# One-core backbone block: modulation rows as unsplit products on four column quarters, re-queued pieces, reordered head work, x loaded first

## The chip, the cores and the metric

The kernel runs on one NeuronCore of one Trainium2 chip. The metric is device time in microseconds (us), lower is better. The kernel before takes 2216.18 us, the median of three runs (2215.4 to 2218.75).

## What is computed

Two layers of a diffusion backbone over 256 context tokens and 512 latent tokens, 1024 channels wide, in float32. Both layers read six modulation vectors (shift, scale and gate, twice), made from a conditioning vector `c` for the latent tokens and `c_ctx` for the context tokens:

```python
def adaln(cvec, w, b):                       # w: (1024, 6144) per layer
    m = jax.nn.silu(cvec) @ w + b
    return jnp.split(m[:, None, :], 6, axis=-1)

for i in range(DEPTH):                       # DEPTH = 2
    sh1, sc1, g1, sh2, sc2, g2 = adaln(c, ada_w[i], ada_b[i])
    hl = modulate(rms_norm(xl, norm1_g[i]), sh1, sc1)      # h * (1 + scale) + shift
    # layer 0: gated linear recurrence of 8 heads, forward and backward (hgrn2_mixer)
    # layer 1: windowed attention with sinks (window_gqa_mixer)
    xl = xl + g1 * ol
    xl = xl + g2 * conv_ffn(modulate(rms_norm(xl, norm2_g[i]), sh2, sc2), ...)
    # the context tokens take the same steps in layer 0
return rms_norm(xl, final_norm_g)
```

The modulation weights are 2 x 1024 x 6144 floats, 48 MB of the traffic. The kernel holds them as 24 rows (12 in each layer) of 512 outputs; a row has four pieces, and a piece has two blocks of 128 inputs by 512 outputs.

## The kernel before, in words

Activations lie with channels on the partitions and tokens along the row. A large product goes over 204 weight tiles of 1024 x 128 channels: 40 for the eight recurrence heads (five for each), 8 for the mixer's output, 68 for the feed-forward of layer 0, then 12, 8 and 68 in layer 1. Each weight tile is read into one of three raw buffers `WR`, split on ScalarE into a high part `WH` (L787) and on VectorE into the rest `WL` (L1086), both in the one-pass type fp32r. TensorE makes three products for each block (L400 to L402): high by high, high by low and low by high. Products of plain float32 operands also occur (L527, L713, L722). The trace shows each of these as two MATMUL records, so its counts are twice the program's.

Every engine runs its own instruction list in order and waits on semaphores. SyncE's list holds all loads: it issues the load of weight tile t once `tile_done` says that tile t-3 was used, and `PIECES` says how many modulation pieces are loaded behind each tile's load. A raw piece arrives as two halves of 128 x 512 in two buffers `ada_raw`. GpSimd splits each half into `ada_high` (L357) and `ada_low` (L359). The load of the next half waits in SyncE's list for `piece_split`, so every later load in that list stands behind it.

A recurrence head is one head step. On TensorE it has ten half tiles of the *next* head's projection (numbered n = 0 to 9, 24 products of 384 columns each). Between them come the products of the current head: eight rounds of scores (level -1 behind n = 2, level k behind n = k + 3; L525 and L527), the key-value products and outputs of the head before (n = 0 and 1), its norm (sums at n = 2, `spread` L498 at n = 3), and the modulation products (L453, L454; n = 5 to 8) with the turn of a finished row into a column (L446, n = 9). Each round of scores waits until VectorE has taken the one before out of PSUM (`take`, L1294). VectorE's list for a head step is: forget gates, states of the head before, `head_out` of the head before (L1317, L1319; it waits for `spread`), the take of level -1, then for each level merging of keys (L1255, L1256), merging of queries (L1266, L1267), take, totals (L1282), with the weight splits `split_low` between them. The eighth head step has no projection of a next head; the mixer's output products fill it.

The feed-forward of layer 0 does the other 12 modulation rows, one piece in the middle of each tile (`ada_tiles`). At the start of the kernel the first four rows are read in `AD0`, split by ScalarE, VectorE and GpSimd (L938, L1143, L373) and multiplied (L479), before the first norm and the first tiles.

One modulation row before: `silu_p` holds the high and the low part of both conditioning vectors, 4 columns in all. For each of the 8 blocks there are two one-pass products, 16 in all, which write 4 partitions of `MB`. ScalarE copies them to `ada_row`, and four small products with `fold` add the parts and put the row across the partitions.

Of the kernel before, what the change touches and what calls it, by code (L numbers as in the profile page):

```python
# [19 lines left out]
F32 = mybir.dt.float32  # L20
# [78 lines left out]
def trunk(nc, small_in, x_in, ada_in, w_in, ident_in, masks_in, rope_in, rot_in, tri_in, out):  # L99
    ctx = ExitStack()  # L100
    with ctx:
# [15 lines left out]
        AR = [sb(f"ada_raw{i}", [P, 512]) for i in range(2)]  # L117
        AH = [sb(f"ada_high{i}", [P, 512], F32R) for i in range(2)]
        AL = [sb(f"ada_low{i}", [P, 512], F32R) for i in range(2)]
# [5 lines left out]
        silu_c = sb("silu_c", [P, KC, 2])  # L125
        sig_c = sb("sig_c", [P, KC, 2])
        silu_p = sb("silu_p", [P, KC, 4], F32R)
        ada_row = sb("ada_row", [4, 512])
        fold = sb("fold", [4, 2])
# [22 lines left out]
        with ExitStack() as s:  # L152
            AD0 = sb("AD0", [P, 4 * ADA_FIRST, 1024], F32, s)
        with ExitStack() as s:
# [11 lines left out]
            O1 = sb("O1", [P, TOK], F32, s)  # L166
            KL = [sb(f"KL{i}", [P, TOK], F32, s) for i in range(2)]
        with ExitStack() as s:
            GH = sb("GH", [P, max(GROUPS), TOK], F32R, s)
            GL = sb("GL", [P, max(GROUPS), TOK], F32R, s)  # L170
            UW = (GRID_H + 2) * (GRID_W + 2)
            UP = [sb(f"UP{i}", [P, UW + CTX + 2], F32, s) for i in range(2)]
            ACC = [sb(f"ACC{i}", [P, TOK], F32, s) for i in range(2)]
        with ExitStack() as s:
# [10 lines left out]
            rope = sb("rope", [P, 2, LAT], F32, s)  # L185
# [23 lines left out]
        ada0_in = [sem(f"ada0_in{i}") for i in range(4 + ADA_FIRST - 1)]  # L209
        ada0_hi, ada0_lo, ada0_lo_pool, ada0_used = sem("ada0_hi"), sem("ada0_lo"), sem("ada0_lo_pool"), sem("ada0_used")  # L210
        w_in_done = [sem(f"w_in_done{i}") for i in range(NB)]
        piece_in = [sem(f"piece_in{i}") for i in range(2)]
# [3 lines left out]
        piece_hi, piece_split = sem("piece_hi"), sem("piece_split")  # L216
        piece_used = sem("piece_used")
        sig_ready, silu_ready, lb_shifted = sem("sig_ready"), sem("silu_ready"), sem("lb_shifted")
        ada_copied, ada_turned, ada_ready = sem("ada_copied"), sem("ada_turned"), sem("ada_ready")
# [20 lines left out]

        BACK, FORE = 0, 1

# [16 lines left out]

        def first_part(t, n):  # L260

            return t[:, :, :].rearrange("p c t -> p (c t)")[:, 1024 * (n % 6):1024 * (n % 6 + 1)]
# [44 lines left out]
        def _(sp):  # L307
            sp.dma_start(small[:, :], small_in).then_inc(small_in_done, 16)
            for n in range(4):
                sp.dma_start(AD0[:, n, :], ada_in[n]).then_inc(ada0_in[n], 16)  # L310
            sp.dma_start(ident[:, :], ident_in).then_inc(ident_in_done, 16)
            for g in range(1, ADA_FIRST):
                sp.dma_start(AD0[:, 4 * g:4 * g + 4, :], ada_in[4 * g:4 * g + 4].rearrange("n p f -> p n f")).then_inc(ada0_in[3 + g], 16)
                if g == 1:
                    sp.dma_start(X[:, :, :], x_in).then_inc(x_in_done, 16)
            sp.dma_start(mask_stage, masks_in).then_inc(masks_in_done, 16)

            raw = Tally()
# [29 lines left out]
        def _(pool):  # L348
            pieces = Tally()

            def split_piece():
                for f in range(2):
                    pieces.add()
                    pool.wait_ge(piece_in[f], pieces.half(0, 16))
                    if pieces.some(2):
                        pool.wait_ge(piece_used, pieces.now(2))
                    pool.tensor_scalar(AH[f][:, :], AR[f][:, :], 1.0, 0.0, ALU.mult, ALU.add).then_inc(piece_hi, 1)  # L357
                    pool.wait_ge(piece_hi, pieces.now())
                    pool.tensor_tensor(AL[f][:, :], AR[f][:, :], AH[f][:, :].bitcast(F32), ALU.subtract).then_inc(piece_split, 1)  # L359

# [9 lines left out]
            for g in range(ADA_FIRST):  # L370
                p = 4 * g + 3
                pool.wait_ge(ada0_hi, p + 1)
                pool.tensor_tensor(first_part(HL, p), AD0[:, p, :], first_part(HH, p).bitcast(F32), ALU.subtract).then_inc(ada0_lo_pool, 1)  # L373
            for n in range(4 * ADA_FIRST, 4 * ADA_GROUPS):
                split_piece()
                if n == 4 * ADA_FIRST + 28:
                    split_heads()

        @block.tensor
        def _(pe):  # L380
# [60 lines left out]
            def ada_turn():  # L441
# [3 lines left out]
                for m in range(4):  # L445
                    last = mm(MB[:, 512 + 2 * m:514 + 2 * m], ada_row[:, m * P:(m + 1) * P], fold[:, :], start=True, stop=True)  # L446
                last.then_inc(ada_turned, 1)

            def ada_piece(k):
                for f in range(2):  # L450
                    pieces.add()
                    pe.wait_ge(piece_split, pieces.now())
# [1160 lines left out]
```

## Time and profile before

| | |
|---|---|
| time, median of 3 runs | 2216.18 us |
| time of the profiled execution | 2217.54 us |
| its span, first to last instruction | 2215.5 us |
| TensorE matmul busy | 2034.7 us, 92% |
| VectorE busy | 1305.8 us, 59% |
| ScalarE busy | 704.2 us, 32% |
| GpSimd busy | 395.8 us, 18% |
| mean granted TensorE clock | 0.946 of full speed |

The profiled execution has 2.0 us outside its span. In the profile PE is TensorE's matmul, PEld its weight load, DVE VectorE, ACT ScalarE, POOL GpSimd and SPq the list of loads. A matmul's duration includes the time in the pipeline, so the start-to-start distance of two neighbours is what one costs in a row.

### The profile page before, as it was taken

To read this page: it belongs to the slowest core of one execution; us is meant where nothing else is said; L and a number is where in the kernel's file an instruction comes from. 1 tells how busy PE (TensorE), PEld (TensorE's weight loads), DVE (VectorE), ACT (ScalarE), POOL (GpSimd) and SP (SyncE) were. 2 spreads that over 40 slices of the span, in tenths; PEclk is the share of its full clock that TensorE was granted. 3 is DMA by queue.
4 is the path that set the end of the run, shared out by engine and by line. 5 is a ranking of instruction groups with operands and counts; after the bars stand their busy time and mean duration, and the time that the engine had idled before them with its cause. 6 is when DMAs were issued, how large, how long until landed. Compare 5 with 4: busy or idle time off the path is not lost.

```text
span 2215.5 us, 26437 instructions
## 1 busy us (share of the span) xinstructions
PE 2034.7 (92%) x10776; PEld 1695.0 (77%) x10776; DVE 1305.8 (59%) x2043; ACT 704.2 (32%) x1065; POOL 395.8 (18%) x342
## 2 busy tenths in 40 slices
PE   5999989899978889999999999799899879999997
PEld 2989889888877768888888888675565567777775
DVE  5555465474566367744774376575355468568485
ACT  5323322323322233221232133345335333233232
POOL 1021222122062004533553352000000000000000
PEclk7999989999989989999999999899989999999998
DMA  6121211212110113323333233210010022232232
GB/s 254 48 76 53 72 58 49 75 48 76 49 58 29 57 52 101 114 95 96 114 104 96 95 111 89 71 58 1 14 44 1 29 76 85 85 94 89 86 95 95
DMA packets 56856, 165.85 MB, mean 75 GB/s; under 512 B 6176, under 2 KB 6560, under 8 KB 56608
## 3 DMA queue, kind: packets, MB, share of 16 engines
q1 hardware_dynamic: 56736, 164.17, 23.3%
q8 instruction: 85, 1.39, 0.3%
q14 instruction: 35, 0.29, 0.0%
HBM read 162.05 MB, written 2.10 MB: 74 GB/s over the span
## 4 chain that ended last, share of the span: by engine, by line
PE 73%; DVE 16%; ACT 4%; DMA 3%; issue 2%; POOL 1%; SPq 0%; DVEq 0%; POOLq 0%
PE slot L400 18%; PE slot L402 17%; PE slot L401 17%; DVE ACC L1403 6%; PE MA L527 4%; PE slot L722 3%; DVE WL L1086 3%; DMA WR<-in_w 2%; PE MB L453 2%; PE MB L454 1%; ACT WH L787 1%; PE slot L713 1%; PE MB L498 1%; PE MB L446 1%; DMA AD<-in_ada 1%
## 5 line engine op out<-in xcount | busy, mean ns | idle before, releaser
L400 PE MATMUL slot<-HH,WH 128*128 128x256 f32 (+2 forms) x2016 | 724.8, 360 | 42.8 <-DVE ACC L1411 14.1
L401 PE MATMUL slot<-HL,WH 128*128 128x256 f32 (+2 forms) x2016 | 710.8, 353 | 0.0
L402 PE MATMUL slot<-HH,WL 128*128 128x256 f32 (+2 forms) x2016 | 710.2, 352 | 0.0
L400 PEld LDWEIGHTS slot<-HH,WH 128*128 128x128 f32 x2016 | 388.3, 193 | 106.6 <-issue 49.1
L1086 DVE TENSOR_TENSOR WL<-WR,WH 128x1024 fp32r<-128x1024 f32 x204 | 292.1, 1433 | 278.4 <-ACT WH L787 276.8
L401 PEld LDWEIGHTS slot<-HL,WH 128*128 128x128 f32 x2016 | 388.1, 193 | 41.4 <-issue 2.2
L402 PEld LDWEIGHTS slot<-HH,WL 128*128 128x128 f32 x2016 | 386.3, 192 | 38.4
L787 ACT ACTIVATE WH<-WR 128x1024 fp32r<-128x1024 f32 x204 | 215.1, 1055 | 415.8 <-DMA WR<-in_w 415.6
L1403 DVE SCALAR_TENSOR_TENSOR ACC<-UP,cw,ACC 128x512 f32<-128x512 f32 x352 | 291.9, 829 | 8.6
L357 POOL TENSOR_SCALAR ada_high<-ada_raw 128x512 fp32r<-128x512 f32 x160 | 129.1, 807 | 904.1 <-DMA ada_raw<-in_ada 454.5
L359 POOL TENSOR_TENSOR ada_low<-ada_raw,ada_high 128x512 fp32r<-128x512 f32 x160 | 236.7, 1479 | 13.3
L400 PE MATMUL slot<-GH,WH 128*128 128x512 f32 (+1 forms) x528 | 192.0, 364 | 8.4 <-DVE GL L1416 8.4
L402 PE MATMUL slot<-GH,WL 128*128 128x512 f32 (+1 forms) x528 | 190.9, 362 | 0.0
L401 PE MATMUL slot<-GL,WH 128*128 128x512 f32 (+1 forms) x528 | 190.5, 361 | 0.0
L527 PE MATMUL MA<-QQ,KL 128*128 128x128 f32 x672 | 102.8, 310 | 51.2 <-DVE PS L1294 51.1
L527 PEld LDWEIGHTS MA<-QQ,KL 128*128 128x128 f32 x672 | 96.9, 219 | 56.1 <-issue 56.0
L400 PEld LDWEIGHTS slot<-GH,WH 128*128 128x128 f32 x528 | 100.5, 190 | 27.0 <-DVE GL L1416 9.7
L991 ACT ACTIVATE ACC<-ACC 128x768 f32<-128x768 f32 (+1 forms) x44 | 32.5, 739 | 272.3 <-DVE ACC L1403 272.3
L401 PEld LDWEIGHTS slot<-GL,WH 128*128 128x128 f32 x528 | 100.7, 191 | 16.8
L402 PEld LDWEIGHTS slot<-GH,WL 128*128 128x128 f32 x528 | 100.7, 191 | 16.5
L873 ACT ACTIVATE KL<-KK 128x384 f32<-128x384 f32 x112 | 53.3, 524 | 127.8 <-DVE KK L1256 124.1
L722 PE MATMUL slot<-PT,AV 128*64 128x512 f32 x144 | 74.8, 670 | 1.4 <-ACT PT L1033 1.4
(182 smaller groups left out, 2159.9 us busy)
## 6 DMA issues: line engine op xcount, KB each, us to landing
WR<-in_w SPq DMA_DIRECT2D x204, 512.0 KB, 3.6
ada_raw<-in_ada SPq DMA_DIRECT2D x160, 256.0 KB, 2.6
AD<-in_ada SPq DMA_DIRECT2D x3, 2048.0 KB, 22.9
X<-in_x SPq DMA_DIRECT2D x1, 3072.0 KB, 19.2
AD<-in_ada SPq DMA_DIRECT2D x4, 512.0 KB, 7.0
out<-Y SPq DMA_DIRECT2D x8, 256.0 KB, 2.2
Y<-in_masks SPq DMA_DIRECT2D x1, 512.0 KB, 25.6
rope<-in_rope SPq DMA_DIRECT2D x1, 512.0 KB, 3.4
```

The source lines that it names most:

```text
L357: pool.tensor_scalar(AH[f][:, :], AR[f][:, :], 1.0, 0.0, ALU.mult, ALU.add).then_inc(piece_hi, 1)
L359: pool.tensor_tensor(AL[f][:, :], AR[f][:, :], AH[f][:, :].bitcast(F32), ALU.subtract).then_inc(piece_split, 1)
L400: mm(SLOT[s][:, po], WH[w % NB][:, k, :], hi[:, k, to], start=(k == 0), stop=False)
L401: mm(SLOT[s][:, po], WH[w % NB][:, k, :], lo[:, k, to], start=False, stop=False)
L402: last = mm(SLOT[s][:, po], WL[w % NB][:, k, :], hi[:, k, to], start=False, stop=(k == kn - 1))
L453: mm(MB[0:4, 0:512], silu_p[:, 2 * k + f, :], AH[f][:, :], start=(k == 0 and f == 0), stop=False)
L527: last = mm(MA[:, chunk(c)], KL[n % 2][:, t], of_level(QQ[b], c * P, P, 2 ** n), start=True, stop=True)
L722: last = mm(SLOT[1][64 * half:64 * half + 64, 0:512], AV[:, c, 64 * half:64 * half + 64], PT[v % 2][:, j, :, :].rearrange("p r q -> p (r q ...
L787: go(WH[t % NB][:, :, :], WR[t % NB][:, :, :], ACT.Copy).then_inc(w_hi_done, 1)
L873: last = go(k, half(KK[b], plane, s, plane), ACT.Copy)
L1086: tt(WL[t % NB][:, :, :], WR[t % NB][:, :, :], WH[t % NB][:, :, :].bitcast(F32), ALU.subtract).then_inc(w_split, 1)
L1403: ins = stt(acc, lat[:, dy:dy + GRID_H, dx:dx + GRID_W], cw[b][:, k:k + 1], acc, ALU.mult, ALU.add)
```

## The change

1. **Unsplit products.** `silu_w` holds the two conditioning vectors in float32, in columns 0 and 1 of 32, the rest zero. A row is 8 plain float32 products of a 128 x 32 stationary operand with a 128 x 512 block. Blocks 0 to 3 write the four column quarters of the array, partitions 0, 32, 64 and 96 of `MB`, and blocks 4 to 7 add to them. `fold`, now 128 x 2, adds the quarters in the turn. GpSimd's splits and `piece_split` are gone, and GpSimd keeps `split_heads` only.
2. **Re-queued pieces.** A piece is one load of 128 x 1024 into one of four buffers, it waits for `pair_used` (TensorE's use of the pair that the buffer held), and is queued behind other tiles: in a head step two pieces each behind two neighbouring tile loads. TensorE does a pair of pieces at once: n = 6 and n = 8 of a head step, and every other tile in the feed-forward.
3. **Start.** x is loaded first, then the pieces. The squares of x are made before the rows, and the norm's sums and reciprocal between the third row and the fourth. `split_low` of the first three tiles moves behind the first scaled chunk. The splits of the first four rows are gone.
4. **Head step.** `head_out` moves from ahead of the take of level -1 (the masked copy of the diagonal scores, `take(LEVELS)`) to behind `merge_keys(0)`. The buffer `O1` is gone; `V` takes its place.

```diff
-            after, n, t = {}, 4 * ADA_FIRST, 7
+            after, n, t = {}, 4 * ADA_FIRST, 5
             for h in range(HEADS - 1):
-                for j in range(5):
-                    after[t + j - 1] = 2 * (j in (2, 3))
+                after[t + 1], after[t + 2] = 2, 2
                 t += 5
-            after[t - 1] = 4
+            after[t + 1], after[t + 2] = 2, 2
...
             def load_piece(n):
-                for f in range(2):
-                    if raw.some(1):
-                        sp.wait_ge(piece_split, raw.now(1))
-                    raw.add()
-                    sp.dma_start(AR[f][:, :], ada_in[n, :, f * 512:(f + 1) * 512]).then_inc(piece_in[f], 16)
+
+                i = n - 4 * ADA_FIRST
+                if i >= 4:
+                    sp.wait_ge(pair_used, i // 2 - 1)
+                sp.dma_start(AR[i % 4][:, :, :], ada_in[n].rearrange("p (f o) -> p f o", f=2)).then_inc(piece_in[i % 4], 16)
...
-            def ada_piece(k):
-                for f in range(2):
-                    pieces.add()
-                    pe.wait_ge(piece_split, pieces.now())
-                    mm(MB[0:4, 0:512], silu_p[:, 2 * k + f, :], AH[f][:, :], start=(k == 0 and f == 0), stop=False)
-                    mm(MB[0:4, 0:512], silu_p[:, 2 * k + f, :], AL[f][:, :], start=False, stop=(k == 3 and f == 1)).then_inc(piece_used, 1)
-                if k == 3:
+            def ada_products(src, k):
+
+                for f in range(4):
+                    c = 2 * k + f
+                    last = mm(MB[32 * f:32 * f + 32, 0:512], silu_w[:, c, :], src(f), start=(k == 0), stop=(k == 2))
+                return last
+
+            def ada_pair(k):
+
+                i = pieces.now()
+                pieces.add(2)
+                for j in range(i, i + 2):
+                    pe.wait_ge(piece_in[j % 4], 16 * (j // 4 + 1))
+                ada_products(lambda f: AR[(i + f // 2) % 4][:, f % 2, :], k).then_inc(pair_used, 1)
+                if k == 2:
                     rows.add()
...
-                    if 5 <= n < 9:
-                        ada_piece(n - 5)
+                    if n in (6, 8):
+                        ada_pair(n - 6)
...
                 scaled(0)
+                if early:
+                    split_low(tile.now() + AHEAD)
...
                 if tail:
                     token_rstd(0)
-                    head_out(h - 1)
                 head.add()
                 take(LEVELS)
                 for n in range(LEVELS):
                     merge_keys(b, n)
+                    if tail and n == 0:
+                        head_out(h - 1)
```

SyncE's list, the loads from the first head step on, before (`WR` are weight tiles, `ada_raw` halves of pieces):

```order
16 L331 DMA WR2<-in_w 128x1024 [waits tile_done]
17 L326 DMA ada_raw0<-in_ada 128x512
18 L326 DMA ada_raw1<-in_ada 128x512
19 L326 DMA ada_raw0<-in_ada 128x512 [waits piece_split]
20 L326 DMA ada_raw1<-in_ada 128x512 [waits piece_split]
21 L331 DMA WR0<-in_w 128x1024 [waits tile_done]
22 L326 DMA ada_raw0<-in_ada 128x512 [waits piece_split]
23 L326 DMA ada_raw1<-in_ada 128x512 [waits piece_split]
24 L326 DMA ada_raw0<-in_ada 128x512 [waits piece_split]
25 L326 DMA ada_raw1<-in_ada 128x512 [waits piece_split]
26 L331 DMA WR1<-in_w 128x1024 [waits tile_done]
```

The same place now, with the pieces of the second head step:

```order
22 L325 DMA WR2<-in_w 128x1024 [waits tile_done]
23 L325 DMA WR0<-in_w 128x1024 [waits tile_done]
24 L325 DMA WR1<-in_w 128x1024 [waits tile_done]
25 L325 DMA WR2<-in_w 128x1024 [waits tile_done]
26 L320 DMA ada_raw0<-in_ada 128x1024 [waits pair_used]
27 L320 DMA ada_raw1<-in_ada 128x1024 [waits pair_used]
28 L325 DMA WR0<-in_w 128x1024 [waits tile_done]
29 L320 DMA ada_raw2<-in_ada 128x1024 [waits pair_used]
30 L320 DMA ada_raw3<-in_ada 128x1024 [waits pair_used]
31 L325 DMA WR1<-in_w 128x1024 [waits tile_done]
```

Before, WR0 and WR1 (rows 21 and 26) stand behind halves that wait for a split. Now the loads in front of a weight tile wait for a pair's products alone.

VectorE's list at the start of the second head step, before (`O1`, `Y` are the output of the head before, `PS` the scores, `KK1` and `QQ1` keys and queries):

```order
149 L1159 RECIPROCAL rstd6<-std6 128x6 [waits std_ready]
150 L1317 TENSOR_TENSOR O1<-O1,MB 128x768 [waits rstd_spread]
151 L1319 TENSOR_TENSOR Y<-Y,O1 128x768 [waits dve_step]
152 L1294 COPY_PREDICATED PS<-masks,MA 128x384 [waits scores_read,scores_done]
153 L1294 COPY_PREDICATED PS<-masks,MA 128x384
154 L1255 TENSOR_TENSOR KK1<-KK1,FD1 128x384 [waits keys_mixed,dve_step]
155 L1256 TENSOR_TENSOR KK1<-KK1,FD1 128x384
156 L1266 TENSOR_TENSOR QQ1<-QQ1,FD1 128x384 [waits scores_done]
```

And now:

```order
141 L1114 RECIPROCAL rstd6<-std6 128x6 [waits std_ready]
142 L1265 COPY_PREDICATED PS<-masks,MA 128x384 [waits scores_read,scores_done]
143 L1265 COPY_PREDICATED PS<-masks,MA 128x384
144 L1226 TENSOR_TENSOR KK1<-KK1,FD1 128x384 [waits keys_mixed,dve_step]
145 L1227 TENSOR_TENSOR KK1<-KK1,FD1 128x384
146 L1288 TENSOR_TENSOR V<-V,MB 128x768 [waits rstd_spread]
147 L1290 TENSOR_TENSOR Y<-Y,V 128x768 [waits dve_step]
148 L1237 TENSOR_TENSOR QQ1<-QQ1,FD1 128x384 [waits scores_done]
```

The take and the first merge of keys no longer stand behind the wait for `rstd_spread`.

## Rows read from the trace of the kernel before

**Rows 1.** The page: busy times, and the chain that ended last, by engine.

```profile
PE 2034.7 (92%) x10776; PEld 1695.0 (77%) x10776; DVE 1305.8 (59%) x2043; ACT 704.2 (32%) x1065; POOL 395.8 (18%) x342
PE 73%; DVE 16%; ACT 4%; DMA 3%; issue 2%; POOL 1%; SPq 0%; DVEq 0%; POOLq 0%
```

**Rows 2.** Stretches: length, busy by engine, clock, DMA share, GB/s.

```profile
16.00:34.00 18.00, 8.90 (x29) 4.55 (x30) 8.12 (x8) 11.43 (x14) 4.33 (x2) 0.62 1.00 409
144.00:620.00 476.00, 433.82 (x2726) 412.86 (x2725) 262.86 (x487) 144.54 (x212) 96.14 (x97) 0.95 0.19 60
620.00:644.00 24.00, 20.12 (x117) 18.18 (x116) 14.60 (x26) 6.48 (x12) 12.85 (x14) 0.93 0.35 109
664.00:690.00 26.00, 22.81 (x149) 20.41 (x147) 16.52 (x29) 6.83 (x11) 5.49 (x5) 0.93 0.00 1
690.00:710.00 20.00, 15.42 (x91) 11.74 (x90) 18.59 (x34) 3.29 (x7) 10.46 (x10) 0.91 0.25 79
800.00:1420.00 620.00, 616.23 (x3455) 519.86 (x3453) 384.43 (x444) 164.24 (x209) 233.46 (x192) 0.99 0.32 98
```

**Rows 3.** TensorE's waits in 144:620, then 620:690: total, times, longest.

```profile
PE MA L527 <- DVE PS L1294: 40.7, 12, 4.3
...
PE MA L527 <- DVE PS L1294: 7.0, 2, 3.9
```

**Rows 4.** Timeline of SyncE's list: start, length, what, count.

```profile
146.08 2.30 SPq L326 DMA_DIRECT2D ada_raw<-in_ada  x2
148.42 34.29 SPq L331 DMA_DIRECT2D WR<-in_w  x4
```

**Rows 5.** Timeline, VectorE and TensorE, first kind of stall.

```profile
153.52 1.52 DVE L1086 TENSOR_TENSOR WL<-WR,WH 128x1024 fp32r<-128x1024 f32 x1 [6.78 <-ACT WH L787]
...
158.03 2.90 PE L527 MATMUL MA<-QQ,KL 128*128 128x128 f32 x12 [3.57 <-DVE PS L1294]
167.24 1.50 PE L527 MATMUL MA<-QQ,KL 128*128 128x128 f32 x12
```

**Rows 6.** Timeline, VectorE and TensorE, second kind of stall.

```profile
198.35 0.95 DVE L1317 TENSOR_TENSOR O<-O,MB 128x768 f32<-128x768 f32 x1 [6.48 <-PE MB L498]
...
200.22 1.04 DVE L1294 COPY_PREDICATED PS<-masks,MA 128x384 f32<-128x384 uint8 x2
...
201.40 2.90 PE L527 MATMUL MA<-QQ,KL 128*128 128x128 f32 x12 [3.09 <-DVE PS L1294]
```

**Rows 7.** Timeline, TensorE, a modulation piece between two half tiles.

```profile
930.04 0.40 PE L453 MATMUL MB<-ada_high,silu_p 128*4 128x512 f32 x1
930.27 0.39 PE L454 MATMUL MB<-ada_low,silu_p 128*4 128x512 f32 x1
...
930.73 0.40 PE L454 MATMUL MB<-ada_low,silu_p 128*4 128x512 f32 x1
930.97 0.40 PE L400 MATMUL slot<-HH,WH 128*128 128x512 f32 x1
```

**Rows 8.** The chain in order of time: plain float32 products of 512 columns.

```profile
1513.71 3.58 PE slot L722 x8
1525.40 4.43 PE slot L722 x10
```

**Rows 9.** Timeline of the start, TensorE, VectorE and ScalarE.

```profile
28.52 3.90 ACT L938 ACTIVATE HH<-AD 128x1024 fp32r<-128x1024 f32 x4 [3.54 <-DMA AD<-in_ada]
45.39 0.59 ACT L945 ACTIVATE ada_row<-MB 4x512 f32<-4x512 f32 x1 [3.46 <-PE MB L479]
47.12 0.17 DVE L1126 TENSOR_TENSOR ada<-MB,small 128x8 f32<-128x8 f32 x1 [2.35 <-PE MB L446]
49.14 3.49 DVE L1086 TENSOR_TENSOR WL<-WR,WH 128x1024 fp32r<-128x1024 f32 x3
55.96 2.19 DVE L1181 SCALAR_TENSOR_TENSOR Y<-X,coef,MB 128x256 f32<-128x256 f32 x4 [3.02 <-PE MB L498]
59.58 0.66 PE L400 MATMUL slot<-HH,WH 128*128 128x384 f32 x1 [3.66 <-DVE HL L1188]
```

More of the change, by code:

```diff
@@ L116, in trunk @@
         WH = [sb(f"WH{i}", [P, KC, P], F32R) for i in range(NB)]
[L117 to L119 removed]
+        AR = [sb(f"ada_raw{i}", [P, 2, 512]) for i in range(4)]
         ident = sb("ident", [P, P])
@@ L173, in trunk @@
             ACC = [sb(f"ACC{i}", [P, TOK], F32, s) for i in range(2)]
+            row2 = sb("row2", [P, 512], F32, s)
         with ExitStack() as s:
@@ L368, in split_heads @@
                     pool.tensor_tensor(HL[:, h, :], Y[:, h, :], HH[:, h, :].bitcast(F32), ALU.subtract).then_inc(early_lo, 1)
[L370 to L377, printed above, removed]
+            split_heads()
         @block.tensor
@@ L445, in ada_turn @@
                 for m in range(4):
-                    last = mm(MB[:, 512 + 2 * m:514 + 2 * m], ada_row[:, m * P:(m + 1) * P], fold[:, :], start=True, stop=True)
+                    last = mm(MB[:, 512 + 2 * m:514 + 2 * m], ada_row(rows.now(1))[:, m * P:(m + 1) * P], fold[:, :], start=True, stop=True)
                 last.then_inc(ada_turned, 1)
-            def ada_piece(k):
-                for f in range(2):
-                    pieces.add()
-                    pe.wait_ge(piece_split, pieces.now())
-                    mm(MB[0:4, 0:512], silu_p[:, 2 * k + f, :], AH[f][:, :], start=(k == 0 and f == 0), stop=False)
-                    mm(MB[0:4, 0:512], silu_p[:, 2 * k + f, :], AL[f][:, :], start=False, stop=(k == 3 and f == 1)).then_inc(piece_used, 1)
-                if k == 3:
+            def ada_products(src, k):
[10 more added lines that the diff above has]
+                if k == 2:
                     rows.add()
@@ L463, in ada_tiles @@
                         half_tile(j % 2, 0, hi, lo, kn)
[L464 removed]
+                        if j % 2:
+                            ada_pair(j - 1)
                         half_tile(j % 2, 1, hi, lo, kn)
                     ada_turn()
[L468 to L486 removed]
             def token_sums(src, first, dst=MA):
@@ L506, in norm_pe @@
                 spread(first)
+            pe.wait_ge(silu_ready, 1)
+            for g in range(ADA_FIRST):
+                pe.wait_ge(ada0_in[g], 16 if g else 64)
+                for k in (0, 2):
+                    if g == 0:
+                        last = ada_products(lambda f: AR[k + f // 2][:, f % 2, :], k)
+                    else:
+                        last = ada_products(lambda f: AD0[:, 4 * g - 4 + k + f // 2, f % 2, :], k)
+                last.then_inc(ada0_used, 1)
+                rows.add()
+                if g == 0:
+                    pe.wait_ge(fold_ready, 1)
+                ada_turn()
+                if g == ADA_FIRST - 2:
+                    sums.add(KC - 1)
+                    pe.wait_ge(sq_added, sums.now())
+                    token_sums(SSQ, 0)
+            pe.wait_ge(ada_ready, rows.now())
+            spread(0)
             level, head, scored, mixed = Tally(), Tally(), Tally(), Tally()
@@ L836, in ada_copy @@
                 rows.add()
-                act.wait_ge(piece_used, rows.times(8, -8 * ADA_FIRST))
-                go(ada_row[:, :], MB[0:4, 0:512], ACT.Copy).then_inc(ada_copied, 1)
+                act.wait_ge(pair_used, rows.times(2, -2 * ADA_FIRST))
+                go(ada_row(rows.now(1))[:, 0:512], MB[:, 0:512], ACT.Copy).then_inc(ada_copied, 1)
             rows = Tally(ADA_FIRST)
@@ L1159, in token_rstd, with norm_dve @@
                 nc.vector.reciprocal(rstd6[:, first:NCH], std6[:, first:NCH]).then_inc(rstd_ready, 1)
-            def norm_dve(tokens, gain, scale, shift):
+            dve.wait_ge(ident_in_done, 16)
+            link(tt(fold[:, :], ident[:, 0:2], ident[:, 32:34], ALU.add))
+            link(tt(fold[:, :], fold[:, :], ident[:, 64:66], ALU.add))
+            tt(fold[:, :], fold[:, :], ident[:, 96:98], ALU.add).then_inc(fold_ready, 1)
+            for c in range(KC):
+                add_square(c, TOK)
+            for g in range(ADA_FIRST):
+                rows.add()
+                ada_add(4 * g)
+                if g == ADA_FIRST - 2:
+                    token_rstd(0)
+            def norm_dve(tokens, gain, scale, shift, early=False):
                 t = slice(TOK - tokens, TOK)
@@ L1165, in norm_dve @@
                     dve.wait_ge(ada_ready, rows.now())
-                    split_low(tile.now() + AHEAD)
+                    if not early:
+                        split_low(tile.now() + AHEAD)
                     link(stt(coef[:, :, :], ada[:, scale:scale + KC, :], 1.0, gain.unsqueeze(2).to_broadcast([P, KC, 2]), ALU.add, ALU.mult))
-                token_rstd((TOK - tokens) // P)
+                if not early:
+                    token_rstd((TOK - tokens) // P)
                 dve.wait_ge(rstd_spread, stats.now())
@@ L1190, in norm_dve @@
                 scaled(0)
+                if early:
+                    split_low(tile.now() + AHEAD)
                 for c in range(KC):
```

128 lines of the change are left out of this document (36 added, 92 removed).

## The prediction

> **What bounds the kernel now.** I read the page first. TensorE's matmuls are busy for 92% of the span and carry 73% of the chain that ended last; VectorE has 16% of the chain [rows 1]. So what counts is TensorE's work, its idle time and its clock. Next I took the busy time by stretches [rows 2]. The feed-forward of layer 0 (800 to 1420 us) has 616.2 us busy of 620 at clock 0.99: there only TensorE's own work counts. Six head steps (144 to 620 us) have 433.8 busy of 476 at a mean clock of 0.95. That is where time is lost.
>
> TensorE's waits name the place: in those six head steps the scores (L527) wait 12 times for `take` on VectorE, 40.7 us in all, and twice more, 7.0 us, in 620 to 690 us [rows 3]. Two waits in each step, of two kinds, read from the timelines:
>
> - **Behind the loads.** VectorE is idle for 6.78 us until 153.52, waiting for the high part of a weight tile. SyncE's list shows why: two loads of halves stand at 146.08, and the next weight tiles go out at 148.42, right behind them [rows 4, 5]. That tile is the first of the next head; its buffer came free two half tiles earlier. VectorE's in-order list holds the take of level 4 behind this split, so TensorE waits 3.57 us, until 158.03 [rows 5].
> - **Behind `head_out`.** VectorE waits 6.48 us for `spread`, then works at `head_out` until 200.2, and only then takes the diagonal scores. TensorE's next scores wait 3.09 us [rows 6].
>
> After both the clock has dropped to its lower level: 12 score records take 2.90 us at 158.03 and 201.40, and 1.50 at 167.24 [rows 5, 6].
>
> **The change part by part.** The sum is made against the profiled execution, 2217.5 us (span 2215.5 and 2.0 around it); the median of the runs is 1.4 lower.
>
> *Loads.* A weight tile now stands behind at most two piece loads that wait for `pair_used`. Four buffers give these a whole head step: the first two pieces of head h need the pair that head h-1 used at n = 6, and are queued behind a tile load that itself waits for that step's n = 7. So the first kind of stall goes. What is late next: the weight tile after it, whose buffer comes free only behind n = 7. If its load goes out at 148.42, where the late one did, its split starts near 153.5 and ends near 155, as the late one's did [rows 4, 5]. VectorE may wait there for a microsecond or two, but this split stands behind the take of level 4 in its list, and TensorE has half tile n = 8 to do, so TensorE does not wait.
>
> *Head step.* The diagonal take now stands ahead of `head_out`, so level 0 may start right behind `spread`. `head_out`'s two operations of 0.95 us end near 200.3, and TensorE first needs them (`y_ready`) behind half tile n = 4, near 204. They delay the merge of queries by 2 us, which half tile n = 4 (24 products of 384 columns; at 0.23 us for 512 [rows 7] that is 0.17 each, 4.1 us) covers. If that cover were gone, it would cost up to 2 us a head step, 14 in all.
>
> Idle time that goes: 40.7 + 7.0 = 47.7 us [rows 3]. Clock that comes back, as the share of a stretch below full speed: 476 x 0.05 = 23.8, 24 x 0.07 = 1.7, 26 x 0.07 = 1.8, together 27.3 us [rows 2]. Bounds: nothing of the clock returns if a gap of another kind remains in each step; all of it if none does, which I take. Sum: -75.0 us.
>
> *GpSimd.* In the last head step (690 to 710 us) VectorE is busy for 18.59 of 20 us while GpSimd splits, TensorE is idle for 4.6 and loses 1.8 by its clock [rows 2]. The splits go. I take half of 6.4: -3 us, with bounds 0 and -6.4. In the feed-forward TensorE waits for nothing, so a freer GpSimd is worth nothing there.
>
> *The rows.* A row was 16 one-pass products at 0.23 us start to start, 3.68 us [rows 7]. Now it is 8 plain float32 products. One such product of 512 columns is two records, and the chain shows 8 records in 3.58 and 10 in 4.43 us: 0.43 us for a record, 0.86 for a product [rows 8]. In a row with no overlap, 8 x 0.86 = 6.88 us, +3.2 a row. What this trace doesn't show is two products in different column quarters side by side: L722 writes one half of the columns several times running. Bounds: no overlap, 6.88; four at once, two pairs of 0.86, 1.72.
>
> I take the value between, from the order of records. If records start in the order of the list, the second record of quarter 0 must wait for the first (same columns, 0.43 us), the first of quarter 1 may start with the second of quarter 0, and so on. Then each product costs 0.43 us and a pair of pieces 4 x 0.43 + 0.43 = 2.15, a row 4.30: +0.62. There are 12 rows in the feed-forward and 8 in the head steps: 20 x 0.62 = +12.4 us.
>
> The Trainium skill (TensorE: Matmul & The Clock Gate, Part 3) says that matmuls start and end strictly in program order, and that three column tiles of 512 columns gave 2.38 times. The first sentence speaks for my staggering. By the second alone a pair would be an estimated 3.44 / 2.38 = 1.45 us and a row 2.9, 28 us better than my sum; no row here shows either.
>
> Switching between a narrow and a full product may cost something. Before, 0.24 us lie between the last narrow product and the next wide one, as between two narrow ones [rows 7]: nothing to be seen, and I take 0. The bound above is the part of a matmul that lies behind its start-to-start distance, 0.39 - 0.23 = 0.16 us, at both ends of 40 pairs: +12.8. The Trainium skill (TensorEngine Tiling (Array Packing), Key Properties) states that changing the tiling mode drains the engine; rows 7 don't show it for a product of 4 columns, and whether 32 at partitions 32 to 96 differ no row says. If it holds, the bound applies.
>
> *Start.* Bytes and rate are the same (409 GB/s, DMA share 1.00) [rows 2], so x would land near 14 us, the four rows' pieces near 18, 23, 28.5 and 33.6: in order behind x, where the third group was there at 28.52 before [rows 9]. A row costs 8 x 0.43 + 0.43 = 3.9 us. Copy and turn take 1.7 us (from the copy's start at 45.39 to 47.12 [rows 9]) and 0.4 for the last product's tail, 2.1. The first row would cost 3.9 more at the lower clock throughout; I take 2.3, as a part of it will. The norm's sums are 12 records, 1.5 us as 12 of the scores. Rows one after the other from 18.2: 18.2 + 4 x 6.0 + 2.3 + 1.5 = 46.0, `ada` of row 4 at 46.3 (before: 47.12), `spread` done 1.5 later at 47.8. Then a scaled chunk 1.1, three weight splits 3.5, a second scaled chunk and its low part 2.3: first tile near 55, against 59.58 [rows 9]. I take -4.5 us. With no overlap of quarters 4 x 3.0 more, +7.5; with four at once the last load is the limit, about -11.
>
> **Sum:** 2217.5 - 75.0 - 3 + 12.4 - 4.5 = 2147.4 us; as the median of runs, 1.4 less: 2146 us.
>
> **The rivals.**
>
> *A. No overlap of the quarters.* For it: no row shows any. Against: the operands use different columns and different output partitions. Then 2217.5 - 78 + 20 x 3.2 + 7.5 = 2211, as a median 2210: the heads' gain is spent on the rows.
>
> *B. Four quarters at once.* For it: eight independent streams by pairs. Against: both records of a product use the same columns, and four streams of float32, each at half the rate of a one-pass product (0.43 against 0.23 us for 512 columns [rows 7, 8]), would need twice what one one-pass product reads. 2217.5 - 78 - 20 x 1.96 - 11 = 2089, median 2088. The page's 2.38 (TensorE: Matmul & The Clock Gate, the Trainium skill) would lie between this and my forecast, near 2118.
>
> *C. Slower: no overlap, and a drain at every switch.* One mechanism: the narrow float32 products run one by one, and each pair is fenced by the tail of the pipeline on both sides. A's 2211 and 12.8 give 2224, median 2222. A's row costs 6.88 us, and from (78 - 7.5) / 20 = 3.5 us above the old 3.68, 7.2 us, the kernel is slower; 0.3 us a row is enough. For it: the bound above. Against: rows 7.
>
> *D. The stalls don't go*, since VectorE or a load is late elsewhere in each head step. VectorE has 262.9 busy of 476 us [rows 2], which speaks against it. Half of the 75 left: 2217.5 - 37.5 - 3 + 12.4 - 4.5 = 2185, median 2183.5.
>
> **How the numbers follow.** Forecast 0.50 (own range 2128 to 2160: above it the cost of switching, below it the start and GpSimd at their better bounds and a pair at 1.8 us), A 0.20, B 0.15, C 0.08, D 0.07. The range leaves out B's 2088 and C: 2098 to 2211. What can be told from no change is 0.2%, 4.4 us: 2211.8 to 2220.6. Faster takes the forecast, B, D and half of A, with room for an A just under the bound, 0.86; within 0.2%, 0.06; slower 0.08.
>
> **What the changed profile would show.** The waits of the scores for the take fall from 47.7 us to under 8, and the clock from 144 us to the end of the head steps is at least 0.98; a head step has the length of about 69 us instead of 79. The loads of `WR` follow each other without a wait on a pair. In a pair of pieces the eight records start about 0.43 us apart two by two: 2.1 us from the first to the next wide product is my case, 3.4 is A, under 1.5 is B, and a gap of 0.16 around it is C. The first tile starts near 55 us. GpSimd is busy for under 40 us. I am wrong if pairs take over 3 us, or if the head step stays above 74 us.

## The result, and the profile after

| | before | changed |
|---|---|---|
| time, median of 4 runs | 2215.80 us | 2097.94 us |
| profiled execution | 2217.54 us | 2097.79 us |
| its span | 2215.5 us | 2096.0 us |

The changed kernel takes 0.9466 of the time before (95% interval 0.9450 to 0.9483). The forecast was 2146 us, with a range from 2098: the result lies at the low end, just outside, and 10 us above rival B (2088).

The page of the changed kernel, the lines that answer to [rows 1]:

```profile
PE 1961.0 (94%) x10776; PEld 1640.8 (78%) x10776; DVE 1192.7 (57%) x2032; ACT 690.3 (33%) x1049; POOL 22.4 (1%) x18
...
PE 78%; DVE 14%; ACT 4%; DMA 2%; issue 2%; SPq 0%; DVEq 0%
```

TensorE is busy for 74 us less although its count of records is the same, 10776: a row was 16 one-pass products and is 8 products of two records. GpSimd fell from 395.8 to 22.4 us.

Stretches of the changed kernel (length, busy by engine, clock, DMA share, GB/s), to be read beside [rows 2]: a stretch within the head steps (6.4 of the new ones; the 476 us of [rows 2] are six of the old) and the feed-forward of layer 0.

```profile
129.00:559.00 430.00, 428.52 (x2889) 413.25 (x2888) 258.72 (x521) 151.97 (x224) 0.23 (x1) 1.00 0.21 72
...
707.00:1312.00 605.00, 593.98 (x3458) 502.62 (x3457) 321.89 (x446) 168.40 (x211) 0.00 (x0) 0.99 0.31 103
```

In the head steps TensorE is busy for 428.5 of 430 us at full clock; before, it was 433.8 of 476 at 0.95. Its waits for `take` were 40.7 us in six steps and 7.0 behind them [rows 3]; now the whole kernel has 1.9:

```profile
PE MA L510 <- DVE PS L1265: 1.9, 2, 1.2
```

VectorE's timeline around the wait for `spread`, to be read beside [rows 6], with TensorE's next scores:

```profile
184.08 0.95 DVE L1288 TENSOR_TENSOR V<-V,MB 128x768 f32<-128x768 f32 x1 [3.56 <-PE MB L461]
185.06 0.96 DVE L1290 TENSOR_TENSOR Y<-Y,V 128x768 f32<-128x768 f32 x1
186.07 0.56 DVE L1237 TENSOR_TENSOR QQ<-QQ,FD 128x384 f32<-128x384 f32 x1
...
183.88 2.15 PE L510 MATMUL MA<-QQ,KL 128*128 128x128 f32 x12
```

The scores start at 183.88, before `head_out` at 184.08; before, they waited until `head_out` and the take were over. The other stall's place, beside [rows 5]: the split of the weight tile that I expected to be late next.

```profile
143.51 1.05 DVE L1265 COPY_PREDICATED PS<-masks,MA 128x384 f32<-128x384 uint8 x2
144.46 0.30 DVE L1253 TENSOR_TENSOR FD<-FD 128x24 f32<-128x24 f32 x2
145.96 1.22 DVE L1059 TENSOR_TENSOR WL<-WR,WH 128x1024 fp32r<-128x1024 f32 x1 [1.20 <-ACT WH L769]
...
146.55 1.50 PE L510 MATMUL MA<-QQ,KL 128*128 128x128 f32 x12
```

VectorE waits 1.20 us for that tile, as forecast, and TensorE's scores at 146.55 don't wait, since the take is ahead.

A pair of pieces between two half tiles, beside [rows 7]. TensorE's timeline:

```profile
880.80 0.28 PE L377 MATMUL slot<-GH,WL 128*128 128x256 f32 x1
881.01 1.07 PE L428 MATMUL MB<-ada_raw,silu_w 128*32 128x512 f32 x8
882.01 0.50 PE L375 MATMUL slot<-GH,WH 128*128 128x512 f32 x1
882.34 0.39 PE L376 MATMUL slot<-GL,WH 128*128 128x512 f32 x1
```

Eight records, 1.00 us from the first to the next wide product. My forecast had 2.1, A 3.4, B under 1.5. The same timeline asked in two narrow stretches of another pair shows how they stand: in 135.84 to 135.88 us only four have started, in 136.24 to 136.26 all eight.

```profile
135.75 0.64 PE L428 MATMUL MB<-ada_raw,silu_w 128*32 128x512 f32 x4
...
135.75 1.07 PE L428 MATMUL MB<-ada_raw,silu_w 128*32 128x512 f32 x8
```

Four records go at once, and the second four about 0.43 us later. The two groups stream for 0.86 us. The rest is for changing over, in three places: 0.21 us from the last wide product to the pair, where 0.12 is usual for its 256 columns; 1.00 - 0.86 = 0.14 within the pair; and 0.33 from the next wide product to the one behind it, where 0.23 is usual. That makes some 0.33 us a pair, 0.66 a row.

**Where 119.5 us of span went.** The chains of the two kernels give the same marks: the first tile, the norm behind the head steps (L498, now L461), the norm ahead of layer 1. One row's saving is the distance of turns over four equal tiles, 916.83 - 878.61 before and

```profile
778.75 0.79 PE MB L421 x8
815.41 0.79 PE MB L421 x8
```

now, in the chain: 36.67 against 38.21, so 1.55 us a row and a net cost of 3.72 - 1.55 = 2.17. Not all of it is in the products: the turn got cheaper too. One turn between its wide products, TensorE's timeline, before and now:

```profile
954.72 0.39 PE L402 MATMUL slot<-HH,WL 128*128 128x512 f32 x1
955.04 1.05 PE L446 MATMUL MB<-fold,ada_row 4*128 4x2 f32 x8
956.02 0.38 PE L400 MATMUL slot<-GH,WH 128*128 128x256 f32 x1
956.24 0.28 PE L401 MATMUL slot<-GL,WH 128*128 128x256 f32 x1
```

```profile
851.69 0.39 PE L377 MATMUL slot<-HH,WL 128*128 128x512 f32 x1
851.92 0.95 PE L421 MATMUL MB<-fold,row 128*128 128x2 f32 x8
852.73 0.36 PE L375 MATMUL slot<-GH,WH 128*128 128x256 f32 x1
852.93 0.28 PE L376 MATMUL slot<-GL,WH 128*128 128x256 f32 x1
```

From the first start to the last it is 1.52 us before and 1.24 now. So the products of a row went from 3.72 us to 1.72 + 0.66 = 2.38, and the turn gave 0.28: together 1.62, against 1.55 by the distance of turns.

| stretch | before | now | difference | forecast |
|---|---|---|---|---|
| start to first tile | 59.58 | 54.06 | -5.5 | -4.5 |
| head steps and mixer output | 733.1 | 642.9 | -90.2: stalls and GpSimd -77.8, 8 rows -12.4 | -78, rows +5.0 |
| feed-forward of layer 0 | 637.7 | 615.1 | -22.6: 12 rows -18.6, rest -4.0 | rows +7.4 |
| layer 1 | 785.1 | 783.9 | -1.2 | 0 |

### The profile page after: what moved, and what is told of

It reads as the page before. It is cut to its first block, busy times and chain, and to the rows that moved or that the text cites. A ratio compares the mean times of both kernels' runs of the same rounds, so it can differ in the third digit from the quotient of the medians.

```text
span 2096.0 us, 25879 instructions
## 1 busy us (share of the span) xinstructions
PE 1961.0 (94%) x10776; PEld 1640.8 (78%) x10776; DVE 1192.7 (57%) x2032; ACT 690.3 (33%) x1049; POOL 22.4 (1%) x18
## 4 chain that ended last, share of the span: by engine, by line
PE 78%; DVE 14%; ACT 4%; DMA 2%; issue 2%; SPq 0%; DVEq 0%
PE slot L375 20%; PE slot L377 19%; PE slot L376 19%; DVE ACC L1375 6%; PE MA L510 4%; PE slot L704 3%; DVE WL L1059 3%; PE MB L428 3%; PE slot L695 2%; ACT WH L769 1%; DMA WR<-in_w 1%; PE MB L461 1%; PE MB L421 1%; DVE ACC L1383 1%; DMA ada_raw<-in_ada 1%
## 5 line engine op out<-in xcount | busy, mean ns | idle before, releaser
L1059 DVE TENSOR_TENSOR WL<-WR,WH 128x1024 fp32r<-128x1024 f32 x204 | 249.3, 1223 | 246.0 <-ACT WH L769 244.4
L1375 DVE SCALAR_TENSOR_TENSOR ACC<-UP,cw,ACC 128x512 f32<-128x512 f32 x352 | 263.9, 750 | 8.6
L510 PE MATMUL MA<-QQ,KL 128*128 128x128 f32 x672 | 90.4, 285 | 2.2 <-DVE PS L1265 1.9
L510 PEld LDWEIGHTS MA<-QQ,KL 128*128 128x128 f32 x672 | 86.7, 192 | 4.6 <-issue 4.5
L1237 DVE TENSOR_TENSOR QQ<-QQ,FD 128x384 f32<-128x384 f32 x56 | 32.6, 582 | 75.8 <-PE MA L510 75.5
L1265 DVE COPY_PREDICATED PS<-masks,MA 128x384 f32<-128x384 uint8 x128 | 67.6, 582 | 13.7 <-PE MA L508 13.7
```

Of the source, the lines that this page charges most:

```text
L510: last = mm(MA[:, chunk(c)], KL[n % 2][:, t], of_level(QQ[b], c * P, P, 2 ** n), start=True, stop=True)
L1059: tt(WL[t % NB][:, :, :], WR[t % NB][:, :, :], WH[t % NB][:, :, :].bitcast(F32), ALU.subtract).then_inc(w_split, 1)
L1265: last = nc.vector.copy_predicated(PS[:, t].rearrange("p (c t) -> p c t", t=P), masks[:, n:n + 1, :].to_broadcast([P, NCH // 2, P]), MA[:, ...
L1375: ins = stt(acc, lat[:, dy:dy + GRID_H, dx:dx + GRID_W], cw[b][:, k:k + 1], acc, ALU.mult, ALU.add)
```

## The experiments

### Which quarters run side by side

e1 puts all products in quarter 0. Copy and turn read 32 partitions (64 in e2 and e3). `FIRST` and `LAST` hold the first and the last block that each used quarter gets.

```diff
-                    last = mm(MB[32 * f:32 * f + 32, 0:512], silu_w[:, c, :], src(f), start=(k == 0), stop=(k == 2))
+                    q = 0              # e2: f % 2, e3: f // 2
+                    last = mm(MB[32 * q:32 * q + 32, 0:512], silu_w[:, c, :], src(f), start=(c in FIRST), stop=(c in LAST))
```

> The changed kernel with all eight products of a row in column quarter 0 (copy and turn read 32 partitions). Nothing can run side by side. A pair of pieces should cost 4 products x 0.86 = 3.44 us and some 0.2 at its ends, a row 7.2 us instead of 2.2: 20 rows x 5.0 = +100 us, and 10 to 25 us at the start. 2208 to 2225 us. If the changed kernel's gain did not come from products side by side, it stays near 2098.

Measured: 2216.86 us, ratio to the kernel before 1.0008 (0.9986 to 1.0030). e2 uses two quarters in turn.

> The changed kernel with the blocks of a pair in quarters 0, 1, 0, 1. Theory L (my forecast: records start in the order of the list, the second record of a product waits for its first): a pair costs 5 x 0.43 = 2.15 and 0.2 at the ends, a row 4.7, 20 x 2.5 = +50 and some 10 at the start: 2158. Theory Q (each quarter takes its own records as soon as it is free, whatever other quarters do): two products behind each other in each of two quarters, 1.72 + 0.2, a row 3.8: +33 and 7 at the start, 2138.

Measured: 2129.36 us, ratio 0.9613 (0.9585 to 0.9641). e3 has the same two quarters in blocks.

> The changed kernel with the blocks of a pair in quarters 0, 0, 1, 1. Theory L: the first record of quarter 1 starts with the fourth of quarter 0, 7 x 0.43 = 3.0 and 0.2, a row 6.4, 20 x 4.2 = +84 and 17 at the start: 2199. Theory Q: the order in the list does not matter, as in quarters 0, 1, 0, 1: 2138.

Measured: 2129.86 us, ratio 0.9616 (0.9587 to 0.9646). A pair in e1, in e2 and in e3, each with the next wide product, from TensorE's timelines. e1:

```profile
148.85 3.62 PE L433 MATMUL MB<-ada_raw,silu_w 128*32 128x512 f32 x8
152.41 0.44 PE L375 MATMUL slot<-HH,WH 128*128 128x384 f32 x1
```

e2:

```profile
135.12 1.91 PE L433 MATMUL MB<-ada_raw,silu_w 128*32 128x512 f32 x8
136.97 0.44 PE L375 MATMUL slot<-HH,WH 128*128 128x384 f32 x1
```

e3, and the same pair asked in 137.15 to 137.19 us, when two records have started:

```profile
136.77 1.92 PE L433 MATMUL MB<-ada_raw,silu_w 128*32 128x512 f32 x8
138.62 0.44 PE L375 MATMUL slot<-HH,WH 128*128 128x384 f32 x1
...
136.77 0.63 PE L433 MATMUL MB<-ada_raw,silu_w 128*32 128x512 f32 x2
```

| quarters | pair, us | turns over four tiles, us | a row, its turn against the old one included |
|---|---|---|---|
| 0 (e1) | 3.56 | 42.09 | 7.6 |
| 0, 1, 0, 1 (e2) | 1.85 | 38.59 | 4.1 |
| 0, 0, 1, 1 (e3) | 1.85 | 38.61 | 4.1 |
| 0, 1, 2, 3 | 1.00 | 36.67 | 2.2 |

One product takes 0.86 us alone in its quarter (e1's eight records in 3.56 us, less the change-over), and n quarters do n products in that time. With what they add to the wide products around them, the two pairs of a row take 7.5, 4.1 and 2.4 us in one, two and four quarters: the streaming (6.88, 3.44, 1.72) and 0.6 to 0.7 for changing over, the same each time. The turn of e1 and e2, over 32 and 64 partitions, still takes what it took over 4 before (0.32 us to its first product and 0.98 from there to the next wide one); only the changed kernel's, over all 128, is cheaper, so the table's last row is 0.2 below its products. A row in one quarter costs 7.6 us, not A's 6.88, and eats the whole gain: e1 is as slow as the kernel before. Theory L falls by e3. If records began in the order of the kernel's list, quarter 1 could have begun with the fourth record of quarter 0 at the earliest, and the pair would take 3.2 us. It takes 1.85, as in e2, and two records start together at its beginning. So each quarter goes on with its own records (theory Q). The Trainium skill (TensorE: Matmul & The Clock Gate, Part 3) says that matmuls start and end strictly in program order; by e3 a start in the order of the kernel's list is wrong here, and the measurement decides. Whether the engine passes waiting records or the list was already rearranged when it reached the engine, the trace does not tell: the records carry no number of their product. One sign speaks for passing, and proves nothing: the two quarters' first records start 0.014 us apart in e3 and 0.007 in e2, as if in e3 one record of quarter 0 had stood between them.

### The two stalls, each by itself

e4 puts `head_out` back in the changed kernel; e5 moves it in the kernel before. The edit is the last two hunks of the diff above.

> The changed kernel with head_out again ahead of the take of the diagonal scores, nothing else changed. My forecast priced this wait at 3.1 us idle and about 1.9 us of clock in each of seven head steps: +35 us, 2133. Rival: without the stall behind the loads the wait is covered by something else: below 2105.

Measured: 2127.48 us, ratio 0.9598 (0.9565 to 0.9631).

> The kernel before with head_out moved behind merge_keys(0), nothing else changed. By my forecast seven waits of 3.1 us and about 1.9 us of clock each go: -35 us, 2181. Rival: the stall behind the loads grows by what is saved: no change, 2216.

Measured: 2186.87 us against 2209.52 on that chip, ratio 0.9894 (0.9877 to 0.9910). e6 leaves SyncE's list to the weight tiles and loads the halves from GpSimd's own list:

```diff
             def load_piece(n):
-                for f in range(2):
-                    ...
+                pass
...
+            def load_half(i):
+                if i < 8 * (ADA_GROUPS - ADA_FIRST):
+                    pool.dma_start(AR[i % 2][:, :], ada_in[4 * ADA_FIRST + i // 2, :, i % 2 * 512:(i % 2 + 1) * 512]).then_inc(piece_in[i % 2], 16)
...
                     pool.tensor_tensor(AL[f][:, :], AR[f][:, :], AH[f][:, :].bitcast(F32), ALU.subtract).then_inc(piece_split, 1)
+                    pool.wait_ge(piece_split, pieces.now())
+                    load_half(pieces.now() + 1)
```

> The kernel before with the halves of the pieces loaded from GpSimd's list, each behind the split that frees its buffer, so that no weight tile stands behind a split in SyncE's list. Everything else as before. By my forecast the seven waits of about 3.75 us and about 2.2 us of clock each go: -41 us, 2175. Rival: the place in the list is not the cause (the load itself or VectorE is late): 2210 to 2216.

Measured: 2174.46 us, ratio 0.9834 (0.9815 to 0.9853). e7 has both edits.

> The kernel before with both edits (halves loaded from GpSimd's list, head_out behind merge_keys(0)). If the two waits add, -75 us: 2141. If one hides behind the other, more than 2160.

Measured: 2147.05 us, ratio 0.9714 (0.9698 to 0.9731).

The mean of five head steps (from one key-value product to the one five steps on, in each kernel's chain) leaves out the start and the stretches behind the head steps. It does not leave out what the chips differ by: the row "before" is from another chip than e5 to e7.

| kernel | head step, us | TensorE's waits for `take`, 129 to 600 us |
|---|---|---|
| before | 79.28 | 40.7 (144 to 620) |
| e5, `head_out` moved | 74.53 | 22.3 |
| e6, pieces off SyncE's list | 74.19 | 18.5 |
| e7, both | 69.50 | none |
| changed, `head_out` back (e4) | 71.97 | 18.5 |
| changed | 67.54 | 0.8, once, in the last head step |

The waits in e5 are those behind the loads, in e6 those behind `head_out`, six each; the lines are of e5 and e6 in that order.

```profile
PE MA L527 <- DVE PS L1294: 22.3, 6, 4.4
```

```profile
PE MA L531 <- DVE PS L1298: 18.5, 6, 3.1
```

Moving `head_out` is worth 4.75 us a step (4.4 in e4), freeing the weight tiles' list 5.1, both together 9.8: they add, and each costs 1.4 to 1.5 times its idle time. I had forecast 5.0, 5.9 and 10.7. On one chip, by the medians against its 2209.52, the gains are smaller than I had expected each time: 22.7 us for e5 (expected 35), 35.1 for e6 (41) and 62.5 for e7 (75). Over seven steps that is 3.2, 5.0 and 8.9 a step, so the price of `head_out` is known to some 1.5 us only; that the two add holds by the medians too, 57.7 against 62.5 with intervals of about 4 us each. The last 1.96 us from e7 to the changed kernel are the row, 1.55, and 0.4 that I didn't separate. e7 also shows that the stalls went without GpSimd's splits going: it still makes all of them.

### What stands on the chain of the start

e8 makes the first three splits before the last row is added, and e9 also loads two rows ahead of x, with the squares behind these rows' copies. The edit of e8:

```diff
             for g in range(ADA_FIRST):
+                if g == ADA_FIRST - 1:
+                    split_high(AHEAD)
                 act.wait_ge(ada0_used, g + 1)
...
                 rows.add()
+                if g == ADA_FIRST - 1:
+                    split_low(AHEAD)
                 ada_add(4 * g)
```

> The changed kernel with the first three weight tiles split while the fourth row's products run (ScalarE's part ahead of the last row's copy, VectorE's ahead of the last addition to ada), not behind the first scaled chunk. In the changed kernel VectorE's splits stand on the chain from 48.3 to 51.7 us. If they are what the first tile waits for, it starts 3.4 us earlier, near 50.6: 2094.5. Rival: the weight tiles land too late for it: no change.

Measured: 2094.20 us, ratio 0.9443 (0.9423 to 0.9463).

> As e8, and the pieces of rows one and two are loaded ahead of x, with the squares behind these rows' copies. In the changed kernel TensorE's first product waits for its load until 18.8 us, and the four rows then follow each other at 6.2 us. With two rows done before x is there, row three starts when it lands, near 28, and the fourth's ada comes near 42 instead of 45.3: another 3.4 us, 2091. Rival: the squares come too late and the norm's sums wait, so nothing is won by the order: as e8.

Measured: 2093.23 us, ratio 0.9443 (0.9422 to 0.9463). e10 is the changed kernel and e11 is e8 again, with e12 on one chip.

> The changed kernel itself, unchanged, beside the next two on one chip, as their base: about 2098 us if the chip is like the first one.

Measured: 2100.22 us, ratio 0.9479 (0.9455 to 0.9502).

> The kernel of e8 again, against the changed kernel on one chip. The splits are off the chain of the start: 3 to 4 us less than e10, of which the runs can show only the sign. Rival: what the start wins is lost behind it, no difference.

Measured: 2093.96 us, ratio 0.9466 (0.9439 to 0.9493). The chain did what e8's expectation said. From `ada` of row four to the first tile it was 9.3 us in e10 and is 6.3 in e11, and TensorE's wait fell from 6.91 to 3.74 us. e10, then e11:

```profile
40.32 0.17 DVE L1098 TENSOR_TENSOR ada<-MB,small 128x8 f32<-128x8 f32 x1 [4.46 <-PE MB L421]
49.65 0.66 PE L375 MATMUL slot<-HH,WH 128*128 128x384 f32 x1 [6.91 <-DVE HL L1157]
```

```profile
42.70 0.17 DVE L1100 TENSOR_TENSOR ada<-MB,small 128x8 f32<-128x8 f32 x1 [0.37 <-PE MB L421]
49.05 0.66 PE L375 MATMUL slot<-HH,WH 128*128 128x384 f32 x1 [3.74 <-DVE HL L1161]
```

But the first tile starts only 0.6 us earlier, since `ada` was 2.4 us earlier in e10: in this start TensorE runs at either level of its clock, from execution to execution. The changed kernel's two profiles have `ada` of row four at 45.33 and at 40.32 us. In e11 the copy of row four also stands behind a split that waits for its weight tile, and TensorE waits for it for 1.47 us, 0.73 in e10. The intervals of e10 and e11 overlap, so a gain in time is not shown. In e9 rows one and two were done early, but row three's products wait for their load until 28.45 us. `ada` of row four comes at 42.10, where I had expected it, but e8 has it at 42.42 already, and the first tiles start at 48.99 and 48.38. The rival's time held; late squares, its reason, are not shown.

```profile
28.45 3.64 PE L429 MATMUL MB<-AD,silu_w 128*32 128x512 f32 x16 [8.35 <-DMA AD<-in_ada]
```

### One change-over for a row

e12 is e11 with a row's four pieces multiplied at once; the loads then wait until the whole row before is used.

```diff
-                ada_products(lambda f: AR[(i + f // 2) % 4][:, f % 2, :], k).then_inc(pair_used, 1)
+                ada_products(lambda f: AR[f // 2][:, f % 2, :], 0)
+                ada_products(lambda f: AR[2 + f // 2][:, f % 2, :], 2).then_inc(pair_used, 1)
```

> The kernel of e11 with all four pieces of a row multiplied at once (at n = 8 of a head step, and in the fourth tile of four), not pair by pair. A pair now costs 1.2 us, of which 0.86 is streaming and some 0.2 to 0.3 is spent at the two changes between narrow and wide products. With one change in and out for each row: 20 x 0.25 = -5 us against e11. Rival: the ends cost nothing of their own: as e11. If the pieces now come too late, TensorE waits for ada_raw and it is slower.

Measured: 2100.12 us, ratio 0.9486 (0.9470 to 0.9502); not faster than e11. The 16 records now take 1.86 us to the next wide product, against 2 x 1.00, and a head step has 67.2 us, 0.3 less than the changed kernel: one change-over of 0.33 us gone. But the feed-forward got 6.8 us longer (from 691.03 to 1313.00 between the two norms), and the waits of TensorE in 700 to 1310 us of e12 say why:

```profile
PE MB L421 <- ACT row L823: 6.6, 7, 1.1
```

The row is finished in the fourth tile, and the turn right behind that tile waits for ScalarE's copy, which stands in ScalarE's list. The products ended at the same half tile before; twice as many of them now stand there. Why that makes the copy late was not followed further.

## Why the prediction was wrong, step by step

- **Loads and head step: right as a sum, not term by term.** Forecast -75.0 us for the two kinds of stall and -3 for GpSimd; measured -77.8 for both together (with 1.55 us a row taken off). The waits are gone, the clock is 1.00, and e5, e6 and e7 show each stall by itself and that they add. The single prices a step were 5 to 16% too high (5.0 and 5.9 against 4.75 and 5.1); why, I didn't settle. That the sum fits to 0.2 us is luck in part. In e7 (on another chip), with both stalls gone and GpSimd still splitting, the stretch from the first tile to the norm takes 667.0 us, 66.1 less than before and not 75. The changed kernel takes 24.1 less again, 12.4 of it by the rows; the other 11.7 stand against my -3. In e7's last head step (606 to 661 us) TensorE waits 4.8 us for GpSimd's low parts, 0.6 in the same step before, so e7 doesn't divide the sum cleanly either:

```profile
PE MB L457 <- POOL ada_low L359: 4.8, 3, 1.7
```

- **The rows: the step that failed.** I took +0.62 us a row, from "if records start in the order of the list, the second record of quarter 0 must wait for the first, the first of quarter 1 may start with the second of quarter 0". By e3 that condition does not hold: the products do not start in the order of the kernel's list. A row costs 2.17 us net: the four quarters run at once as in rival B, 1.72, with 0.66 at the changes and 0.28 less in the turn (2.10 by these parts). The difference is 20 x (0.62 + 1.55) = 43 us of the 50 by which the forecast missed (2147.4 against 2097.8).
- **The argument against B fell too.** I held that four float32 streams need twice what a one-pass product reads. Four records started within the same 0.1 us and each still took as long as alone: e1's record distance is that of the changed kernel, 0.43 us.
- **Switching: at my upper bound.** I took 0, with 0.16 at each end as the bound (0.64 a row). Measured: 0.66 a row over the streaming time. For a product of 4 columns [rows 7] there was none, and my 0 rested on that. The drain at a change of tiling that the Trainium skill states (TensorEngine Tiling (Array Packing), Key Properties) agrees with this 0.33 us a pair, no more than that.
- **The turn: a term that I put at nothing, without a reason.** It now reads 128 partitions, not 4, and takes 0.28 us less a row. Without this and with switching at 0.66 the rows would have saved 1.34.
- **C and D.** C would have needed A's row. e1 has C's mechanism, serial products and a price at every switch, and came out as no change, 2216.86 us: 20 rows at 7.6 - 3.72 = 3.9 us cost 78, which is what the stalls and GpSimd gave. D fell with the waits.
- **Start: near in the one execution, and open to chance** (-4.5 against -5.5). The chain depends on the clock from run to run: in e10, the same kernel, the first tile starts at 49.65 us, 9.9 earlier than before, and its time is no shorter (2100.22 us).
- **Feed-forward beside the rows: 4.0 us missed.** I held that a freer GpSimd is worth nothing there, since TensorE waits for nothing. But in the first tiles it does wait for VectorE: 2.9 us before, 1.5 in the changed kernel. Before, GpSimd's splits run beside the last four tap operations ahead of that wait, and these take 4.47 us; now they take 3.11. VectorE and GpSimd before, then VectorE now:

```profile
825.06 4.47 DVE L1403 SCALAR_TENSOR_TENSOR ACC<-UP,cw,ACC 128x512 f32<-128x512 f32 x4
...
825.32 0.96 POOL L357 TENSOR_SCALAR ada_high<-ada_raw 128x512 fp32r<-128x512 f32 x1 [122.31 <-DMA ada_raw<-in_ada]
...
829.08 1.58 POOL L359 TENSOR_TENSOR ada_low<-ada_raw,ada_high 128x512 fp32r<-128x512 f32 x1
```

```profile
729.28 3.11 DVE L1375 SCALAR_TENSOR_TENSOR ACC<-UP,cw,ACC 128x512 f32<-128x512 f32 x4
```

The clock falls right behind the longer wait: it is at 0.92 and 0.86 in the two stretches of 8 us from 826 to 842, a loss of 1.8 us by their shares. e6 and e7 settle it: GpSimd still splits there, but not during these four operations. They take 3.11 us, the wait is 1.5, e6's clock in the same place (792 to 808) is 1.00, and norm to norm takes 634.5 and 634.7 us, 3.2 and 3.0 less than before. That leaves 0.8 to 1.0 of the 4.0 us, not followed.

VectorE's busy time in the tap operations of the feed-forward's stretch (clock, DMA share and GB/s behind it): L1403 before, L1375 after, L1407 in e6.

```profile
800.00:1420.00 620.00, 159.88 (x176) 0.99 0.32 98
```

```profile
707.00:1312.00 605.00, 131.88 (x176) 0.99 0.31 103
```

```profile
766.00:1386.00 620.00, 181.20 (x176) 1.00 0.30 97
```

## What to carry to other kernels

Here narrow products in different column quarters ran side by side in both orders that were tried, so a float32 product that needs no split can be cheaper than two one-pass products of its parts (2.4 us a row against 3.7); the same products in one quarter cost twice as much (7.5). When loads for different users share an in-order list, a load that waits for a slow user holds back every tile behind it, and here TensorE paid 1.4 to 1.5 times such a gap, with what its clock lost. A forecast that hits a sum of several terms has not shown any of them: look at a run that changes one. When a trace can't show whether two things overlap, the order of records is an argument for a bound, not for the value.

## What the runs showed of the hardware that I had not expected

- Four plain float32 products of 512 columns in four quarters take 0.86 us together, each as fast as alone, and all four start within 0.1 us.
- Changing between products 32 and 128 columns wide costs some 0.33 us for a way in and out, with one, two or four quarters in use; between 4 and 128 columns nothing was seen.
- The eight small products of a turn take 0.28 us less with their wide neighbours when they read 128 partitions than when they read 4; with 32 and 64 partitions (e1, e2) they take what they take with 4.
- VectorE's 176 tap operations took 131.9 us with GpSimd idle, 159.9 beside its splits and 181.2 where it also issued the loads (e6). In the later tiles TensorE paid nothing for it: turns over four tiles are 38.21 us apart before and in e6. Where TensorE waited for VectorE, it paid 1.4 us and a stretch at the lower clock.
- Row products in the start ran at either level of the clock in different executions of one kernel: 16 records took 3.64 us (1.2 GHz) or 1.92 us (2.4 GHz), which goes far to explain why the fourth `ada` moved by 5 us. Row three in e10 and in the changed kernel's first profile:

```profile
30.00 1.92 PE L428 MATMUL MB<-AD,silu_w 128*32 128x512 f32 x16
```

```profile
31.16 3.64 PE L428 MATMUL MB<-AD,silu_w 128*32 128x512 f32 x16
```
